# Layer-norm and post-norm ends: statistics per half tile, moments of both tiles ahead of the second normalisation

## The chip, the cores and the metric

One core of one Trainium2 chip. The metric is device microseconds of one execution of the whole program. The kernel before takes 2635.37 us (median of 3 runs, 2634.71 to 2635.55).

## The reference

The program computes two stacks of two layers on 256 tokens of width 1024 (the second stack also carries 256 context tokens), all in float32. The first stack has three layer norms in each layer:

```python
x = layer_norm(ALPHA * x + 0.5 * swiglu(x, gate1, up1, down1), ln1_g, ln1_b)
x = layer_norm(ALPHA * x + hybrid_mixer(x, ..., w_out), ln2_g, ln2_b)
x = layer_norm(ALPHA * x + 0.5 * swiglu(x, gate2, up2, down2), ln3_g, ln3_b)

def layer_norm(x, g, b):
    mu = mean(x); var = mean((x - mu) ** 2)
    return (x - mu) * rsqrt(var + 1e-5) * g + b
```

The second stack adds a branch scaled by a root mean square, after its mixer and after its FFN, for each stream of tokens:

```python
x = x + gate * rms_norm(y, weight)       # rms_norm(y) = y * rsqrt(mean(y * y) + 1e-6) * weight
```

## The kernel before

The program is a chain of phases. A phase gives each engine its own instruction list; the lists are tied by semaphores, and a barrier of all engines closes it (line 205), so that the next phase starts when the last engine is done. Weights and activations of the large products are split into a high and a low float32r part, and each product is made of three: high by high, high by low, low by high.

256 tokens are two tiles of 128 (`TT`). The down product of an FFN phase (`down`, line 544) and the output product of a mixer (`out_phase`, line 1019) collect a tile of 128 tokens by 1024 columns in two PSUM banks of 512 columns: tile 0 in banks 0 and 1, tile 1 in banks 2 and 3. The last step of either goes tile by tile and bank by bank, three products of 512 columns to a bank, 12 in all; after the sixth and the twelfth it raises `tile_done`. This is the start of what is called an end here.

A **layer-norm end** (`ln_vector`, line 315, and `ln_scalar`, line 334) takes one tile after the other. VectorE waits for `tile_done`, takes `bn_stats` of both banks (line 319) and `bn_aggr` (321); ScalarE takes the square root (337); VectorE the reciprocal (323) and the shift -mean/std (326); then VectorE normalises bank 0 of the tile (327) and ScalarE bank 1 (339), both into `z`. Only then does VectorE turn to the statistics of tile 1. TensorE turns `z` by transposes (`turn_tensor`, 350), eight to a tile: the first four wait for VectorE's half (`z0_ready`), the last four for ScalarE's (`z1_ready`). With both tiles turned, ScalarE (343) and VectorE (331) write four pieces each of `x_T`, with gain and bias, and the barrier follows.

There are six such ends: layer by layer an FFN phase, a mixer's output phase and an FFN phase.

A **post-norm end** (`post_scalar`, 378; `post_scale`, 392; `post_add`, 401) has ScalarE square both banks of a tile with a sum (384), take the root (387), and after VectorE's reciprocal (396) scale bank 1 (389) while VectorE scales bank 0 (398). ScalarE comes to tile 1 after that. After the transposes VectorE adds eight pieces to `x_T` (404).

There are six of these too: two in `out_both_phase` and two in `ffn_both_phase` (one for each stream; the first stream's lies under the products of the second, which run on TensorE until its transposes are placed at a fixed place, `BEHIND`), one in `out_phase` and one in the last `ffn_phase`.

SyncE loads the first weights of the next phase (`load_ahead`, 224) during the end, and waits for them before the barrier.

Of the kernel before, what the change touches and what calls it, by code (L numbers as in the profile page):

```python
# [36 lines left out]
ALU = mybir.AluOpType  # L37
ACT = mybir.ActivationFunctionType
# [4 lines left out]
D = 1024  # L43
# [3 lines left out]
TT = S // P  # L47
# [3 lines left out]
BANK = 512  # L51
# [261 lines left out]


def ln_vector(dve, k, s, t, par_g, par_b):
    for tt in range(TT):
        dve.wait_ge(s["tile_done"], tt + 1)
        for n in range(2):
            dve.bn_stats(t.stats[:, tt, n, :], k.ps[:, 2 * tt + n, :]).then_inc(s["ln_stats"], 1)
        dve.wait_ge(s["ln_stats"], 2 * tt + 2)  # L320
        dve.bn_aggr(t.mv[:, tt, :], t.stats[:, tt, :, :]).then_inc(s["ln_mv"], 1)
        dve.wait_ge(s["ln_std"], tt + 1)
        dve.reciprocal(t.rstd[:, tt:tt + 1], t.std[:, tt:tt + 1]).then_inc(s["ln_rstd"], 1)
        dve.wait_ge(s["ln_rstd"], tt + 1)

        dve.scalar_tensor_tensor(t.shift[:, tt:tt + 1], t.mv[:, tt, 0:1], -1.0, t.rstd[:, tt:tt + 1], ALU.mult, ALU.mult).then_inc(s["ln_shift"], 1)
        dve.tensor_scalar(t.z[:, tt, 0:BANK], k.ps[:, 2 * tt, :], t.mv[:, tt, 0:1], t.rstd[:, tt:tt + 1], ALU.subtract,
                          ALU.mult).then_inc(s["z0_ready"], 1)
    for f in (2, 3, 6, 7):
        dve.wait_ge(s["ln_turned"], f // 2 + 1)  # L330
        dve.tensor_scalar(k.x_T[:, f, 0:S], turned(k, f), par_g(f), par_b(f), ALU.mult, ALU.add)


def ln_scalar(act, k, s, t, par_g, par_b):
    for tt in range(TT):
        act.wait_ge(s["ln_mv"], tt + 1)
        act.activation(t.std[:, tt:tt + 1], t.mv[:, tt, 1:2], ACT.Sqrt, bias=k.eps[:, 0:1]).then_inc(s["ln_std"], 1)
        act.wait_ge(s["ln_shift"], tt + 1)
        act.activation(t.z[:, tt, BANK:D], k.ps[:, 2 * tt + 1, :], ACT.Identity, bias=t.shift[:, tt:tt + 1],
                       scale=t.rstd[:, tt:tt + 1]).then_inc(s["z1_ready"], 1)  # L340
    for f in (0, 1, 4, 5):
        act.wait_ge(s["ln_turned"], f // 2 + 1)
        act.activation(k.x_T[:, f, 0:S], turned(k, f), ACT.Identity, bias=par_b(f), scale=par_g(f))


def turned(k, f, bank=4):
    return k.ps[:, bank + f // 2, f % 2 * S:(f % 2 + 1) * S]
# [30 lines left out]
def post_scalar(act, k, s, t, st=0):  # L378
    if st == 0:
        act.activation(t.shift[:, 0:1], k.eps[:, 1:2], ACT.Sqrt)  # L380
    for tt in range(TT):
        made, at = st * TT + tt + 1, 4 * st + 2 * tt
        act.wait_ge(s["tile_done"], made)
        act.activation(t.z[:, tt, :], k.ps[:, at:at + 2, :].rearrange("p b n -> p (b n)"), ACT.Square,
                       accum_out=t.mv[:, tt, 0:1]).then_inc(s["po_sq"], 1)
        act.wait_ge(s["po_sq"], made)
        act.activation(t.std[:, tt:tt + 1], t.mv[:, tt, 0:1], ACT.Sqrt, bias=k.eps[:, 1:2], scale=1.0 / D).then_inc(s["po_std"], 1)
        act.wait_ge(s["po_r"], made)
        act.activation(t.z[:, tt, BANK:D], k.ps[:, at + 1, :], ACT.Copy, scale=t.rstd[:, tt:tt + 1]).then_inc(s["z1_ready"], 1)


def post_scale(dve, k, s, t, st=0):
    for tt in range(TT):
        made, at = st * TT + tt + 1, 4 * st + 2 * tt
        dve.wait_ge(s["po_std"], made)
        dve.reciprocal(t.rstd[:, tt:tt + 1], t.std[:, tt:tt + 1]).then_inc(s["po_r"], 1)
        dve.wait_ge(s["po_r"], made)
        dve.tensor_scalar(t.z[:, tt, 0:BANK], k.ps[:, at, :], t.rstd[:, tt:tt + 1], None, ALU.mult).then_inc(s["z0_ready"], 1)


def post_add(dve, k, s, gain, cols, st=0, bank=4):
# [27 lines left out]
def ffn_phase(nc, k, w_gate, w_up, w_down, src, ln=None, conv=None, post=None, mod=None, loaded=None, ahead=(), reloads=False):  # L429
# [17 lines left out]
    LAST = NF - 1  # L447
    PAIRS = (NF - 8) // 2
    with ExitStack() as ctx:
# [18 lines left out]
        with phase(nc, names) as (block, s):  # L468
# [49 lines left out]
            def _(pe):  # L518
# [25 lines left out]
                def down(t, n, first=False, end=False):  # L544
                    pe.wait_ge(s["dn_split"], t + 1)
                    pe.wait_ge(s["h_ready"], t + 1)
                    for tt in range(TT):
                        for c in range(2):
                            for p, (h, wt) in enumerate(((h_hi, dn_hi), (h_hi, dn_lo), (h_lo, dn_hi))):
                                last = pe.matmul(k.ps[:, 2 * tt + c, :], h[n][:, tt * P:(tt + 1) * P], wt[n][:, c * BANK:(c + 1) * BANK],  # L550
                                                 start=(first and p == 0), stop=(end and p == 2), skip_group_check=True)
                        if end:
                            last.then_inc(s["tile_done"], 1)
                    if not end:
                        last.then_inc(s["down_done"], 1)

# [462 lines left out]
def out_phase(nc, k, chunks, ln=None, post=None, ahead=(), stream=None, raw=None):  # L1019
# [5 lines left out]
    LAST = len(chunks) - 1  # L1025
    SLOTS = 3
    with ExitStack() as ctx:
# [4 lines left out]
        t = ln_buffers(nc, ctx)  # L1032
        if stream is not None:
            chunks = [(y, raw[:, n % SLOTS, :]) for n, y in enumerate(chunks)]
        with phase(nc, names) as (block, s):

            @block.sync
            def _(sp):
                if stream is not None:
                    for n in range(SLOTS):  # L1040
                        sp.sem_inc(s[f"w{n}_in"], 16)
                    for n in range(SLOTS, len(chunks)):
                        sp.wait_ge(s["lo_made"], n - SLOTS + 1)
                        sp.dma_start(raw[:, n % SLOTS, :], stream[n]).then_inc(s[f"w{n % SLOTS}_in"], 16)
                load_ahead(sp, s, ahead)

            @block.tensor
            def _(pe):
                if ln:
                    for tt in range(TT):  # L1050
                        for f in range(FT):
                            pe.matmul(k.ps[:, 2 * tt + f // 4, f % 4 * P:(f % 4 + 1) * P], k.x_T[:, f, tt * P:(tt + 1) * P],
                                      k.alpha[:, :], start=(f % 4 == 0), stop=False, skip_group_check=True)
                for n, (y, _) in enumerate(chunks):
                    rows, m = y.shape[0], n % SLOTS
                    pe.wait_ge(s["lo_made"], n + 1)
                    for tt in range(TT):
                        for c in range(2):
                            for p, (a, b) in enumerate(((y_hi, w_hi), (y_hi, w_lo), (y_lo, w_hi))):
                                last = pe.matmul(k.ps[:, 2 * tt + c, :], a[0:rows, m, tt * P:(tt + 1) * P], b[0:rows, m, c * BANK:(c + 1) * BANK],  # L1060
                                                 start=(n == 0 and p == 0 and not ln), stop=(n == LAST and p == 2), skip_group_check=True)
                        if n == LAST:
                            last.then_inc(s["tile_done"], 1)
                    if n < LAST:
                        last.then_inc(s["chunk_done"], 1)
                turn_tensor(pe, k, s, t.z, s["ln_turned"] if ln else s["po_turned"])

            @block.scalar
            def _(act):
                for n, (y, moving) in enumerate(chunks):  # L1070
                    rows, m = y.shape[0], n % SLOTS
                    if n >= SLOTS:
                        act.wait_ge(s["chunk_done"], n - SLOTS + 1)
                    act.activation(y_hi[0:rows, m, :], y, ACT.Copy)
                    if stream is not None:
                        act.wait_ge(s[f"w{m}_in"], n // SLOTS * 16 + 16)
                    act.activation(w_hi[0:rows, m, :], moving, ACT.Copy).then_inc(s["hi_made"], 1)
                if ln:
                    ln_scalar(act, k, s, t, *ln)
                else:  # L1080
                    post_scalar(act, k, s, t)

            @block.vector
            def _(dve):
                for n, (y, moving) in enumerate(chunks):
                    rows, m = y.shape[0], n % SLOTS
                    dve.wait_ge(s["hi_made"], n + 1)
                    dve.tensor_tensor(y_lo[0:rows, m, :], y, y_hi[0:rows, m, :].bitcast(F32), ALU.subtract)
                    dve.tensor_tensor(w_lo[0:rows, m, :], moving, w_hi[0:rows, m, :].bitcast(F32), ALU.subtract).then_inc(s["lo_made"], 1)
                if ln:  # L1090
                    ln_vector(dve, k, s, t, *ln)
                else:
                    post_vector(dve, k, s, t, *post)
# [1978 lines left out]
```

## Time and profile before

| | before |
|---|---|
| median of 3 runs | 2635.37 us |
| the profiled execution, its time | 2632.28 us |
| its span | 2630.5 us |
| mean granted clock of TensorE | 0.937 of full |
| TensorE busy | 2389.3 us (91%) |
| VectorE busy | 1317.9 us (50%) |
| ScalarE busy | 1135.1 us (43%) |
| GpSimd busy | 140.4 us (5%) |

The span is the profiled execution from its first to its last instruction; its own time has 1.8 us more around it. Busy times overlap. A granted clock of 1.00 is 2.4 GHz, one of 0.5 is 1.2 GHz, and a mean between them says how a stretch is shared between the two.

### The profile page before, as it was taken

How to read it: one execution, taken by the hardware profiler on the slowest of the kernel's cores; microseconds unless marked ns; L12 is line 12 of the kernel's file. 1: busy time of each engine (PE TensorE's matmuls, PEld its weight loads, DVE VectorE, ACT ScalarE, POOL GpSimd, SP SyncE). 2: the span in 40 equal slices, each digit the busy share in tenths (PEclk: the TensorE clock that was granted, in tenths of full speed). 3: DMA queues.
4: the chain of work that ended last, by engine and by line, in shares of the span. 5: the costliest groups of instructions: out<-in, count | busy, mean ns of one | idle time of the engine just before them, and what ended most of it. 6: DMA issues, size and time to landing. Idle time of an engine off the chain costs nothing. (4 is left out here: it accounts for less than half of the span.)

```text
span 2630.5 us, 42098 instructions
## 1 busy us (share of the span) xinstructions
PE 2389.3 (91%) x16488; PEld 2060.9 (78%) x16488; DVE 1317.9 (50%) x2144; ACT 1135.1 (43%) x1996; POOL 140.4 (5%) x177
## 2 busy tenths in 40 slices
PE   7998989998999899999688998769999988986998
PEld 6887978887989787888556887548888777865997
DVE  5443246444544315544444666555555554436665
ACT  3333244333433325443336576434334444434554
POOL 1000001000100000100000212110000000001000
PEclk9999889999999979999799999879999978997999
DMA  7876124885778421587311111124444252204663
GB/s 225 262 247 183 35 65 137 241 251 147 240 248 256 113 65 48 167 254 241 110 39 41 41 50 50 33 61 123 120 120 120 98 143 80 89 1 119 189 180 95
DMA packets 395292, 350.37 MB, mean 133 GB/s; under 512 B 25380, under 2 KB 358552, under 8 KB 394648
## 3 DMA queue, kind: packets, MB, share of 16 engines
q1 hardware_dynamic: 385076, 297.87, 39.4%
q10 hardware_dynamic: 10084, 50.66, 5.4%
q8 instruction: 93, 1.52, 0.2%
q14 instruction: 39, 0.32, 0.0%
HBM read 347.44 MB, written 1.05 MB: 132 GB/s over the span
## 5 line engine op out<-in xcount | busy, mean ns | idle before, releaser
L524 PE MATMUL ps<-x_hi,gu_hi 128*128 128x256 f32 x1680 | 478.9, 285 | 0.0
L524 PE MATMUL ps<-x_hi,gu_lo 128*128 128x256 f32 x1680 | 475.8, 283 | 0.0
L524 PE MATMUL ps<-x_lo,gu_hi 128*128 128x256 f32 x1680 | 475.8, 283 | 0.0
L524 PEld LDWEIGHTS ps<-x_hi,gu_hi 128*128 128x128 f32 x1680 | 322.2, 192 | 22.6 <-DVE gu_lo L669 17.5
L524 PEld LDWEIGHTS ps<-x_lo,gu_hi 128*128 128x128 f32 x1680 | 322.4, 192 | 2.6
L524 PEld LDWEIGHTS ps<-x_hi,gu_lo 128*128 128x128 f32 x1680 | 322.4, 192 | 0.0
L669 DVE TENSOR_TENSOR gu_lo<-w_gu,gu_hi 128x1024 fp32r<-128x1024 f32 x220 | 266.8, 1248 | 87.2 <-ACT gu_hi L600 87.2
L600 ACT ACTIVATE gu_hi<-w_gu 128x1024 fp32r<-128x1024 f32 x220 | 221.9, 1051 | 44.5 <-issue 30.1
L611 ACT ACTIVATE silu<-ps 128x256 f32<-128x256 f32 x88 | 33.7, 383 | 418.0 <-PE ps L524 405.0
L695 DVE SCALAR_TENSOR_TENSOR hid<-silu,ps 128x256 f32<-128x256 f32 x88 | 37.1, 421 | 316.0 <-ACT silu L611 315.8
L550 PE MATMUL ps<-dn_hi,h_hi 128*128 128x512 f32 x440 | 173.8, 395 | 5.9 <-DVE h_lo L704 5.8
L550 PE MATMUL ps<-dn_lo,h_hi 128*128 128x512 f32 x440 | 173.1, 394 | 0.0
L550 PE MATMUL ps<-dn_hi,h_lo 128*128 128x512 f32 x440 | 172.0, 391 | 0.0
L677 DVE TENSOR_TENSOR dn_lo<-w_dn,dn_hi 128x1024 fp32r<-128x1024 f32 x110 | 133.7, 1219 | 10.7 <-ACT dn_hi L604 10.7
L820 PE MATMUL ps<-both_x_lo,gu_hi 128*128 128x512 f32 x336 | 130.8, 389 | 0.0
L820 PE MATMUL ps<-both_x_hi,gu_lo 128*128 128x512 f32 x336 | 130.8, 389 | 0.0
L820 PE MATMUL ps<-both_x_hi,gu_hi 128*128 128x512 f32 x336 | 130.8, 389 | 0.0
L604 ACT ACTIVATE dn_hi<-w_dn 128x1024 fp32r<-128x1024 f32 x110 | 115.1, 1051 | 17.3 <-PE ps L550 17.3
L550 PEld LDWEIGHTS ps<-dn_hi,h_hi 128*128 128x128 f32 x440 | 83.3, 189 | 21.4 <-issue 7.0
L978 DVE SCALAR_TENSOR_TENSOR conv<-ps,par,conv 128x510 f32<-128x510 f32 x44 | 30.9, 745 | 134.4 <-ACT conv L915 134.4
L550 PEld LDWEIGHTS ps<-dn_hi,h_lo 128*128 128x128 f32 x440 | 83.1, 189 | 18.1
L550 PEld LDWEIGHTS ps<-dn_lo,h_hi 128*128 128x128 f32 x440 | 83.4, 189 | 13.4
(419 smaller groups left out, 5191.1 us busy)
## 6 DMA issues: line engine op xcount, KB each, us to landing
w_gu<-in_ffn_w_up SPq DMA_DIRECT2D x178, 512.0 KB, 6.2
w_dn<-in_ffn_w_down SPq DMA_DIRECT2D x134, 512.0 KB, 3.8
w_mod<-in_w_mod ACTq DMA_DIRECT2D x64, 768.0 KB, 6.1
w_gu<-in_ffn_w_gate SPq DMA_DIRECT2D x90, 512.0 KB, 5.1
odd_w<-in_odd_w_qkv SPq DMA_DIRECT2D x24, 512.0 KB, 5.2
w_gu<-in_ffn_w_down SPq DMA_DIRECT2D x11, 1024.0 KB, 5.0
hgrn_w<-in_even_w_in SPq DMA_DIRECT2D x20, 512.0 KB, 3.9
w_in_q<-in_w_in SPq DMA_DIRECT2D x2, 3072.0 KB, 11.2
```

The source lines that it names most:

```text
L524: last = pe.matmul(gu(n)[:, a, :], wt[n][:, a, f, :], x[:, f, :], start=(f == 0 and p == 0), stop=(f == FT - 1 and p == 2), skip_group_che ...
L550: last = pe.matmul(k.ps[:, 2 * tt + c, :], h[n][:, tt * P:(tt + 1) * P], wt[n][:, c * BANK:(c + 1) * BANK], start=(first and p == 0), stop ...
L600: act.activation(gu_hi[n][:, a, :, :], wgu[n][:, a, :, :], ACT.Copy).then_inc(s["w_hi"], 1)
L604: act.activation(dn_hi[n][:, :], wdn[n][:, :], ACT.Copy).then_inc(s["w_hi"], 1)
L611: act.activation(sil[n][:, :], gu(n)[:, 0, :], ACT.Silu).then_inc(s["act_done"], 1)
L669: last = dve.tensor_tensor(gu_lo[n][:, a, :, :], wgu[n][:, a, :, :], gu_hi[n][:, a, :, :].bitcast(F32), ALU.subtract)
L677: dve.tensor_tensor(dn_lo[n][:, :], wdn[n][:, :], dn_hi[n][:, :].bitcast(F32), ALU.subtract).then_inc(s["dn_split"], 1)
L695: dve.scalar_tensor_tensor(hid[n][:, :], sil[n][:, :], 0.5, gu(n)[:, 1, :], ALU.mult, ALU.mult).then_inc(s["h_full"], 1)
L820: last = pe.matmul(gu(n, a), wt[n][:, a, f, :], x[:, f, :], start=(f == 0 and p == 0), stop=(f == FT - 1 and p == 2))
L978: dve.scalar_tensor_tensor(cv[n][:, a, :, 1:S], streams(n, a)[:, :, 0:S - 1], conv.tap(0, t, a), cv[n][:, a, :, 1:S], ALU.mult, ALU.add).t ...
```

## The change

For a layer-norm end, `tile_done` is raised after each bank (four times) and VectorE's list gets another order: the statistics of both banks of tile 0 as they come, the moments of tile 0, the statistics of bank 0 of tile 1, reciprocal and shift of tile 0, statistics of bank 1 of tile 1, the moments of tile 1, and then the normalisation of tile 0, reciprocal and shift of tile 1, its normalisation. ScalarE's order stays as it was. For a post-norm end, `tile_done` stays as it was, and bank 1 of tile 0 is scaled by VectorE, behind bank 0, and not by ScalarE; tile 1 is as before. The post-norm functions serve all six ends.

```diff
 def ln_vector(dve, k, s, t, par_g, par_b):
-    for tt in range(TT):
-        dve.wait_ge(s["tile_done"], tt + 1)
-        for n in range(2):
-            dve.bn_stats(t.stats[:, tt, n, :], k.ps[:, 2 * tt + n, :]).then_inc(s["ln_stats"], 1)
+    def stats(tt, n):
+        dve.wait_ge(s["tile_done"], 2 * tt + n + 1)
+        dve.bn_stats(t.stats[:, tt, n, :], k.ps[:, 2 * tt + n, :]).then_inc(s["ln_stats"], 1)
+
+    def moments(tt):
         dve.wait_ge(s["ln_stats"], 2 * tt + 2)
         dve.bn_aggr(t.mv[:, tt, :], t.stats[:, tt, :, :]).then_inc(s["ln_mv"], 1)
+
+    def scales(tt):
         dve.wait_ge(s["ln_std"], tt + 1)
         dve.reciprocal(t.rstd[:, tt:tt + 1], t.std[:, tt:tt + 1]).then_inc(s["ln_rstd"], 1)
         dve.wait_ge(s["ln_rstd"], tt + 1)
 
         dve.scalar_tensor_tensor(t.shift[:, tt:tt + 1], t.mv[:, tt, 0:1], -1.0, t.rstd[:, tt:tt + 1], ALU.mult, ALU.mult).then_inc(s["ln_shift"], 1)
+
+    def first_half(tt):
         dve.tensor_scalar(t.z[:, tt, 0:BANK], k.ps[:, 2 * tt, :], t.mv[:, tt, 0:1], t.rstd[:, tt:tt + 1], ALU.subtract,
                           ALU.mult).then_inc(s["z0_ready"], 1)
+    for n in range(2):
+        stats(0, n)
+    moments(0)
+    stats(1, 0)
+    scales(0)
+    stats(1, 1)
+    moments(1)
+    first_half(0)
+    scales(1)
+    first_half(1)
...
@@ post_scalar
-        act.wait_ge(s["po_r"], made)
-        act.activation(t.z[:, tt, BANK:D], k.ps[:, at + 1, :], ACT.Copy, scale=t.rstd[:, tt:tt + 1]).then_inc(s["z1_ready"], 1)
+        if tt == TT - 1:
+            act.wait_ge(s["po_r"], made)
+            act.activation(t.z[:, tt, BANK:D], k.ps[:, at + 1, :], ACT.Copy, scale=t.rstd[:, tt:tt + 1]).then_inc(s["z1_ready"], 1)
...
@@ post_scale
         dve.tensor_scalar(t.z[:, tt, 0:BANK], k.ps[:, at, :], t.rstd[:, tt:tt + 1], None, ALU.mult).then_inc(s["z0_ready"], 1)
+        if tt < TT - 1:
+            dve.tensor_scalar(t.z[:, tt, BANK:D], k.ps[:, at + 1, :], t.rstd[:, tt:tt + 1], None, ALU.mult).then_inc(s["z1_ready"], 1)
...
@@ ffn_phase, down (out_phase alike, with n == LAST)
-                        if end:
-                            last.then_inc(s["tile_done"], 1)
+                            if end and (ln or c == 1):
+                                last.then_inc(s["tile_done"], 1)
```

## Rows read from the trace of the kernel before

**Rows 1.** What TensorE waited for before the transposes (line 356): us, times.

```profile
  DVE ln_z_b L327: 44.6, 24
  DVE ln_z_b L398: 18.1, 14
```

**Rows 2.** Timeline, first layer-norm end: start us, us, engine, line, operation [idle before].

```profile
229.37 0.39 PE L550 MATMUL ps<-dn_hi,h_lo 128*128 128x512 f32 x1
...
229.80 1.30 DVE L319 BATCH_NORM_STATS2 ln_stats_b<-ps 128x6 f32<-128x512 f32 x2 [2.36 <-PE ps L550]
...
230.73 0.39 PE L550 MATMUL ps<-dn_hi,h_lo 128*128 128x512 f32 x1
231.13 0.21 DVE L321 BATCH_NORM_AGGREGATE ln_mv_b<-ln_stats_b 128x2 f32<-128x12 f32 x1
231.37 0.29 ACT L337 ACTIVATE ln_std_b<-ln_mv_b,eps 128x1 f32<-128x1 f32 x1 [3.09 <-DVE ln_mv_b L321]
231.70 0.16 DVE L323 RECIPROCAL ln_rstd_b<-ln_std_b 128x1 f32<-128x1 f32 x1 [0.36 <-ACT ln_std_b L337]
231.90 0.16 DVE L326 SCALAR_TENSOR_TENSOR ln_shift_b<-ln_mv_b,ln_rstd_b 128x1 f32<-128x1 f32 x1
231.97 0.81 DVE L327 TENSOR_SCALAR ln_z_b<-ps,ln_mv_b,ln_rstd_b 128x512 f32<-128x512 f32 x1
...
232.70 1.28 DVE L319 BATCH_NORM_STATS2 ln_stats_b<-ps 128x6 f32<-128x512 f32 x2
...
232.83 1.09 PE L356 MATMUL ps<-ident,ln_z_b 128*128 128x128 f32 x8 [1.72 <-DVE ln_z_b L327]
...
234.86 0.81 DVE L327 TENSOR_SCALAR ln_z_b<-ps,ln_mv_b,ln_rstd_b 128x512 f32<-128x512 f32 x1
...
235.72 1.09 PE L356 MATMUL ps<-ident,ln_z_b 128*128 128x128 f32 x8 [1.79 <-DVE ln_z_b L327]
```

**Rows 3.** Timeline, fifth layer-norm end: its transposes, tile 0 and tile 1.

```profile
1062.68 1.91 PE L356 MATMUL ps<-ident,ln_z_b 128*128 128x128 f32 x8 [1.72 <-DVE ln_z_b L327]
...
1065.57 1.97 PE L356 MATMUL ps<-ident,ln_z_b 128*128 128x128 f32 x8 [0.98 <-DVE ln_z_b L327]
```

**Rows 4.** Stretches of four ends: from:to length, busy by engine, clock, DMA, GB/s.

```profile
229.76:238.55 8.79, 3.54 (x22) 2.49 (x21) 6.90 (x16) 4.08 (x8) 0.00 (x0) 1.00 0.01 2
425.91:435.19 9.28, 4.42 (x22) 3.20 (x21) 6.90 (x16) 4.07 (x8) 0.00 (x0) 0.79 0.00 0
...
861.04:869.83 8.79, 3.54 (x22) 2.49 (x21) 6.91 (x16) 4.07 (x8) 0.00 (x0) 0.91 0.00 0
1059.60:1068.89 9.29, 5.24 (x23) 3.86 (x21) 6.91 (x16) 4.07 (x8) 0.00 (x0) 0.67 0.00 0
```

**Rows 5.** The stretch right after the first end, same columns.

```profile
238.60:250.00 11.40, 9.01 (x18) 4.57 (x19) 6.33 (x11) 6.59 (x11) 0.00 (x0) 0.70 0.77 278
```

**Rows 6.** Timeline, post-norm end of `out_both_phase`, second stream.

```profile
1733.41 0.39 PE L2859 MATMUL ps<-both_w_hi,both_y_lo 128*128 128x512 f32 x1
...
1733.62 0.29 ACT L387 ACTIVATE ln_std_b<-ln_mv_b,eps 128x1 f32<-128x1 f32 x1
...
1734.15 0.69 ACT L389 ACTIVATE ln_z_b<-ps,ln_rstd_b 128x512 f32<-128x512 f32 x1 [0.23 <-DVE ln_rstd_b L396]
...
1734.73 1.02 ACT L384 ACTIVATE ln_z_b<-ps 128x1024 f32<-128x1024 f32 x1
...
1736.39 0.75 DVE L398 TENSOR_SCALAR ln_z_b<-ps,ln_rstd_b 128x512 f32<-128x512 f32 x1
```

**Rows 7.** Timeline, three other post-norm ends: a hidden turn, and the squares of tile 1.

```profile
1718.27 1.91 PE L356 MATMUL ps<-ident,ln_z_b 128*128 128x128 f32 x16
...
2136.59 1.02 ACT L384 ACTIVATE ln_z_b<-ps 128x1024 f32<-128x1024 f32 x1 [0.36 <-PE ps L870]
...
2615.95 1.02 ACT L384 ACTIVATE ln_z_b<-ps 128x1024 f32<-128x1024 f32 x1 [0.20 <-PE ps L550]
```

**Rows 8.** Waits of SyncE's queue, 636 to 656 us: total, times, longest.

```profile
SPq L205 <- PEq L205: 3.3, 1, 3.3
```

More of the change, by code:

```diff
@@ L334, in ln_scalar, with deviation, second_half @@
 def ln_scalar(act, k, s, t, par_g, par_b):
-    for tt in range(TT):
+    def deviation(tt):
         act.wait_ge(s["ln_mv"], tt + 1)
         act.activation(t.std[:, tt:tt + 1], t.mv[:, tt, 1:2], ACT.Sqrt, bias=k.eps[:, 0:1]).then_inc(s["ln_std"], 1)
+    def second_half(tt):
         act.wait_ge(s["ln_shift"], tt + 1)
@@ L340, in ln_scalar @@
                        scale=t.rstd[:, tt:tt + 1]).then_inc(s["z1_ready"], 1)
+    for tt in range(TT):
+        deviation(tt)
+        second_half(tt)
     for f in (0, 1, 4, 5):
@@ L1061, in _ @@
                                                  start=(n == 0 and p == 0 and not ln), stop=(n == LAST and p == 2), skip_group_check=True)
-                        if n == LAST:
-                            last.then_inc(s["tile_done"], 1)
+                            if n == LAST and (ln or c == 1):
+                                last.then_inc(s["tile_done"], 1)
                     if n < LAST:
```

## The prediction

> **What bounds the kernel now.** I read the page's busy times first: TensorE is busy 91% of the span, no other engine above 50%, so a stage counts where TensorE has nothing to do. The list of what TensorE waited for before its transposes gives the place: 44.6 us for VectorE's half in layer-norm ends and 18.1 us in post-norm ends [rows 1]. (It counts weight loads and matmuls separately, so about half of that is wall time.) Then the timeline of one end and the stretches of four of them. In the timeline the reader is to see one chain that passes from engine to engine with nothing beside it. From tile 0's last product at 229.76 (229.37 + 0.39) to the last product at 231.12, VectorE starts statistics only at 229.80, having sat idle 2.36 us, and takes them up for tile 1 at 232.70, although that tile has been finished since 231.12 [rows 2]. An end lasts 8.8 to 9.3 us from there to its last write, at 1.00 and 0.91 of the clock 8.79, at 0.79 and 0.67 some 9.28 [rows 4]. Nothing else of the program runs meanwhile, so what the chain loses there the program loses.
>
> **Layer-norm ends, step by step.** Call T the end of the last product, 231.12 here. One bank is three products, 0.68 us (12 of them take 2.72 us by the distance of 1.36 us between 229.37 and 230.73 for six). So the banks are done at T-2.04, T-1.36, T-0.68 and T. Durations from [rows 2]: statistics 0.68 each; two back to back take 1.30, so the second starts 0.62 after the first, 0.06 to 0.07 before that one ends; moments 0.21, root 0.29, reciprocal and shift 0.16, half normalisation 0.81, with VectorE's next instruction 0.73 after its start; a result passes on in 0.03 to 0.04. The new list, as times from T:
>
> - statistics of bank 0 at -2.01, of bank 1 at -1.32 (its bank lands at -1.36) to -0.64; moments -0.60 to -0.39; ScalarE's root -0.36 to -0.07.
> - statistics of bank 2 at -0.46 to 0.23; reciprocal 0.16, shift 0.36, statistics of bank 3 at 0.44 to 1.12.
> - moments of tile 1 at 1.15 to 1.36; ScalarE has normalised bank 1 from 0.55 to 1.33 and does the second root at 1.39 to 1.68.
> - VectorE normalises bank 0 at 1.29 to 2.10; reciprocal 2.02, shift 2.22, bank 2 at 2.30 to 3.11. ScalarE's bank 3 runs 2.42 to 3.20 and is wanted only by the fifth transpose.
>
> Before, the two halves of VectorE ended at T+1.66 and T+4.55, and tile 1's transposes began at 235.72, T+4.60 [rows 2]. After, tile 0's begin at T+2.15, 0.44 later than before, and eight of them take 0.94 us from first to ninth start (1.09 less 0.27 for the last one's own length, over seven, is 0.117 each); tile 1's begin at T+3.15. That is 1.45 us earlier. Everything behind (four pieces on each of ScalarE and VectorE, barrier) is the same, so an end gains 1.45 us at full clock. The two added waits on `tile_done` have nothing queued behind them that could run sooner: each bank's statistics are VectorE's next work. Two more semaphore increments on products cost nothing visible; the one after the sixth product leaves the stream's distance at 0.23 us as elsewhere. That VectorE's next free moment at T+2.02 is 0.3 us after the second root is the part not gained. Bounds for an end: if nothing overlaps on VectorE, 1.0 (below); at the other end, tile 0's turn as early as before (T+1.71) and tile 1's right behind it, at T+2.65, 1.95 earlier than before.
>
> Where the granted clock is low, transposes take 1.91 and 1.97 us for eight, 0.235 each [rows 3]. In the fifth end both tiles were slow: tile 0's eight would run from T+2.15 to T+4.03, and tile 1's start then and not at T+4.60, a gain of 0.57. In the second, third and sixth end only tile 1's were slow, and it costs such an end 0.49 us (9.28 against 8.79) [rows 4]; a turn that ends 1.45 us earlier escapes some of it, if the clock falls at the same moment. I take 0.25 for each of three, with ends 0 and 0.5. Sum: 5 x 1.45 + 0.57 + 0.75 = 8.6 us.
>
> **Post-norm ends.** ScalarE's second tile of squares starts at 1734.73, only because ScalarE first scaled bank 1 of tile 0; tile 1's last product ended at 1733.80 (1733.41 + 0.39) [rows 6]. Without that scaling the squares start at about 1733.84, and tile 1's root is ready at 1735.27 instead of 1736.16 (0.23 ahead of 1736.39, where tile 1's scaling starts). VectorE now scales both banks of tile 0: at 1734.15 and, with the same overlap of 0.07 as its normalisation, 1734.83, and is free at 1735.51. It reaches tile 1's reciprocal then, and its half at 1735.71 instead of 1736.39: 0.68 us gained, the other 0.2 eaten by the added instruction. Tile 0's fifth transpose waits until 1735.6 for the half that moved; with tile 1's at 1736.5 that is covered. The end of `out_phase` has the same times and gains 0.68 as well. The other four give nothing. In the second stream of `ffn_both_phase` and in the last FFN, ScalarE waited for TensorE before tile 1's squares, 0.36 and 0.20 us [rows 7]: it was free already. In the first streams of the two both-phases, the turn starts with no wait behind the other stream's products, all sixteen at once (1718.27 [rows 7]). Sum 1.4 us, ends 0 (if VectorE's second scaling delays as much as ScalarE's removal gains) and 1.8 (two times 0.89).
>
> **Is it passed on?** SyncE waits for the next phase's weights before the barrier; in the third end these had landed 3.3 us before the others came [rows 8], more than the 1.45 to 1.95 us that the others now come earlier; the sixth is alike, and the others had more by the same view. What the next phases issue goes from their start and moves with it.
>
> **The queue's overlap, against the Trainium skill.** The rows show the second statistics 0.62 us after the first, at a length of 0.68, and statistics 0.73 after a normalisation of 0.81 [rows 2]. The Trainium skill (VectorE: DVE Perf Modes, "The DRAIN you can't avoid") says that the next VectorE instruction does not start until the pipe is empty. With each instruction at full length, as by that rule, the list above is 0.46 us longer and an end gains 1.0, six ends 2.8 us less than forecast. I go by the rows; the rule is the first rival.
>
> **The clock.** The granted clock was 1.00 through the first end and 0.70 in the 11.4 us after it [rows 4, 5], and below 1.00 in the other three ends shown [rows 4]: it falls in or behind them. TensorE's idle stretch between last product and first transpose grows from 1.7 to 2.2 us, the one between the two turns nearly goes, and the whole end shrinks. I book nothing for either; the third and fourth rival hold the two sides.
>
> **The sum.** 8.6 + 1.4 = 10.0 us off the profiled execution's 2632.3. That execution lies 3.1 us below the median; the difference carries over, 2635.4 - 10.0 = 2625.4.
>
> **Rivals.**
> 1. No overlap on VectorE, the drain as stated: six ends lose 0.46, two lose 0.2, gain 6.8, 2628.6 us. Against it [rows 2] with two different pairs; for it, that reciprocal behind statistics is a pair that no row shows.
> 2. Half of it is hidden by something that doesn't move: weights that land late at a barrier, or the next phase's first work waiting on its own loads. Gain 4 to 5, 2631 us. For it: SyncE's margin in the third end is only 3.3 us. Against: it is a margin still.
> 3. Slower: the clock. TensorE idles 0.44 us longer before tile 0's transposes, the clock falls behind each of six ends one stretch more than it did, and the next phase's first products run at half speed. After the first end the low share is 0.30/0.5 of 11.4 us, 6.8 us, and half of that time is lost if TensorE is the bound: 3.4 us an end [rows 5], 20.5 in all, 2646 us. It is slower than before from a loss of 1.7 us an end (10.0 over six). Against: four of the six ends run partly at low clock anyway (0.79 and 0.67 in two of those shown), and their cost is already in the time; the three timed executions lie within 0.84 us.
> 4. The ends that ran at low clock come out at full clock once they are shorter: 0.5 us on four ends and 3.4 after one or two of them, 2619 us.
>
> **Numbers.** About 0.2% (5.3 us) is what a measurement tells from no change. Chances: forecast 0.66, no overlap 0.10, half hidden 0.12, clock worse 0.04, clock better 0.08. The forecast's bounds are 6 x 1.0 + 0 = 6 to 6 x 1.95 + 1.8 = 13.5 us, of which I hold 7 to 13 likely. The range 2620.5 to 2631.0 leaves out the clock rivals and half of the second. Faster than 2630.1: 0.85, within 0.2%: 0.11, slower than 2640.6: 0.04.
>
> **What would show it.** In the changed kernel's timeline of a layer-norm end: four statistics, the first about 0.68 us before tile 0's last product; VectorE's first half ending near T+2.1 and the second near T+3.1, TensorE's second turn at T+3.15; the stretch from tile 0's last product to the last write 7.3 us for 8.79. In `out_phase`'s post-norm end: squares of tile 1 right behind the first root, the second turn 0.68 us earlier. Wrong it would be if tile 1's turn waited for ScalarE's half or for tile 0's transposes, if SyncE came last at a barrier, or if the mean clock fell below 0.93.

## The result and the profile after

The changed kernel takes 2617.83 us (median of 6 runs, 2613.33 to 2621.0), beside 2634.16 for the kernel before (6 runs, 2629.96 to 2635.55): ratio 0.9945, 95% interval 0.9934 to 0.9956, or 14.5 us less. Forecast were 10.0 us less and a time of 2625.4 in a range of 2620.5 to 2631.0. The time lies below that range. Two later comparisons of the same two kernels gave 0.9959 and 0.9971. This section and the next say which part of the 14.5 us the change made.

| | before | after |
|---|---|---|
| profiled execution | 2632.28 us | 2618.02 us |
| its span | 2630.5 us | 2615.9 us |
| mean granted clock | 0.937 | 0.942 |
| TensorE busy | 2389.3 us | 2380.4 us |
| VectorE busy | 1317.9 us | 1320.2 us |
| ScalarE busy | 1135.1 us | 1131.4 us |

What TensorE waited for ahead of the transposes, in the kernel after, answers to [rows 1]: us, times.

```profile
  DVE ln_z_b L332: 26.8, 12
  DVE ln_z_b L419: 13.4, 14
  DVE ln_z_b L421: 0.7, 3
```

44.6 us became 26.8 (layer norm) and 18.1 became 14.1 (post norm; line 421 is VectorE's new scaling of tile 0's bank 1); matmuls and weight loads are both counted. The timeline of the sixth layer-norm end of the kernel after shows how; it answers to [rows 2], with T = 1270.57.

```profile
1268.57 1.38 DVE L318 BATCH_NORM_STATS2 ln_stats_b<-ps 128x6 f32<-128x512 f32 x2 [1.68 <-PE ps L573]
...
1269.98 0.21 DVE L322 BATCH_NORM_AGGREGATE ln_mv_b<-ln_stats_b 128x2 f32<-128x12 f32 x1
1270.11 0.65 DVE L318 BATCH_NORM_STATS2 ln_stats_b<-ps 128x6 f32<-128x512 f32 x1
1270.18 0.39 PE L573 MATMUL ps<-dn_hi,h_lo 128*128 128x512 f32 x1
...
1270.67 0.14 DVE L326 RECIPROCAL ln_rstd_b<-ln_std_b 128x1 f32<-128x1 f32 x1
...
1270.92 0.69 DVE L318 BATCH_NORM_STATS2 ln_stats_b<-ps 128x6 f32<-128x512 f32 x1
...
1271.65 0.21 DVE L322 BATCH_NORM_AGGREGATE ln_mv_b<-ln_stats_b 128x2 f32<-128x12 f32 x1
1271.78 0.76 DVE L332 TENSOR_SCALAR ln_z_b<-ps,ln_mv_b,ln_rstd_b 128x512 f32<-128x512 f32 x1
1271.89 0.29 ACT L352 ACTIVATE ln_std_b<-ln_mv_b,eps 128x1 f32<-128x1 f32 x1
1272.45 0.15 DVE L326 RECIPROCAL ln_rstd_b<-ln_std_b 128x1 f32<-128x1 f32 x1
1272.59 2.08 PE L376 MATMUL ps<-ident,ln_z_b 128*128 128x128 f32 x16 [2.02 <-DVE ln_z_b L332]
...
1272.71 0.81 DVE L332 TENSOR_SCALAR ln_z_b<-ps,ln_mv_b,ln_rstd_b 128x512 f32<-128x512 f32 x1
```

The reader is to see VectorE without a pause of more than 0.04 us from 1268.57 on, and sixteen transposes as one group: tile 1's follow tile 0's without a wait. Tile 0's turn starts at T+2.02 (forecast 2.15). The first transpose of tile 1 starts at T+3.01 (forecast 3.15). Not all ends ran like this. The stretches of the first and the sixth end of the kernel after, from tile 0's last product to the last write, answer to [rows 4].

```profile
229.41:237.45 8.04, 4.70 (x23) 3.72 (x21) 6.07 (x16) 4.08 (x8) 0.00 (x0) 0.79 0.00 0
1269.21:1276.42 7.21, 3.44 (x22) 2.49 (x21) 6.08 (x16) 4.08 (x8) 0.00 (x0) 1.00 0.62 174
```

At a granted clock of 1.00 the end takes 7.21 us for 8.79 [rows 4]; where the clock was at half in part of it, 8.04. From T to the last write, the six layer-norm ends took 7.43, 7.93, 7.90, 7.43, 7.92 and 7.91 us before, and 6.68, 6.91, 6.28, 6.20, 6.33 and 5.85 after: 0.75, 1.02, 1.62, 1.23, 1.59 and 2.06 less, 8.3 in all.

The post-norm end of `out_both_phase`, second stream, in the kernel after, answers to [rows 6].

```profile
1723.22 0.29 ACT L407 ACTIVATE ln_std_b<-ln_mv_b,eps 128x1 f32<-128x1 f32 x1
1723.43 1.02 ACT L404 ACTIVATE ln_z_b<-ps 128x1024 f32<-128x1024 f32 x1
...
1723.75 0.75 DVE L419 TENSOR_SCALAR ln_z_b<-ps,ln_rstd_b 128x512 f32<-128x512 f32 x1
...
1724.41 0.74 DVE L421 TENSOR_SCALAR ln_z_b<-ps,ln_rstd_b 128x512 f32<-128x512 f32 x1
...
1725.07 0.15 DVE L417 RECIPROCAL ln_rstd_b<-ln_std_b 128x1 f32<-128x1 f32 x1
...
1725.26 0.75 DVE L419 TENSOR_SCALAR ln_z_b<-ps,ln_rstd_b 128x512 f32<-128x512 f32 x1
1726.07 1.09 PE L376 MATMUL ps<-ident,ln_z_b 128*128 128x128 f32 x8 [0.20 <-DVE ln_z_b L419]
```

ScalarE squares tile 1 right after tile 0's root, and VectorE then is the one that is late. The last product ended at 1723.39, tile 1's turn starts 2.68 after it, 3.40 before: 0.73 us gained, in the end of `out_phase` as well, and nothing (0.01 at most) in the other four.

For the last FFN's end that "nothing" holds only for this pair of traces. In both, the products of tile 1 ran at half clock there, 0.43 us apart and not 0.23, so that ScalarE had time to spare; in the kernel before:

```profile
2614.86 0.63 PE L550 MATMUL ps<-dn_lo,h_hi 128*128 128x512 f32 x1
2615.29 0.63 PE L550 MATMUL ps<-dn_hi,h_lo 128*128 128x512 f32 x1
```

From the last product to the last write this end takes 6.22 us in both. In the traces below in which these products ran at full clock it takes 7.10 with the post-norm functions of before (one trace) and 6.35 to 6.37 with the changed ones (six traces): there it gains 0.7 as well.

SyncE's margin in the third end answers to [rows 8]:

```profile
SPq L205 <- PEq L205: 1.6, 1, 1.6
```

It fell from 3.3 to 1.6 us (from 3.5 to 1.6 in the sixth end, 9.8 or more in the others) and still hid the weights.

So the ends are 8.3 + 1.5 = 9.7 us shorter. The span is 14.6 us shorter. The other 4.9 us come from the stages between, whose code the change does not touch.

### The profile page after: what moved, and what is told of

The parts are those of the page before. It is cut to its first block and busy times, and to the rows that moved or that the text cites. A ratio compares the mean times of both kernels' runs of the same rounds, so it can differ in the third digit from the quotient of the medians.

```text
span 2615.9 us, 42098 instructions
## 1 busy us (share of the span) xinstructions
PE 2380.4 (91%) x16488; PEld 2055.1 (79%) x16488; DVE 1320.2 (50%) x2150; ACT 1131.4 (43%) x1990; POOL 140.7 (5%) x177
```

## The experiments

Each timing is a ratio to the kernel before, run on the same chip, with its 95% interval. "Ends" is the sum, over all twelve, of the time from the last product to the last write, read from that kernel's trace and compared with the trace before. Two theories were put against each other: **A**, that the change gains in the ends and again between them, by the granted clock; **B**, that it gains what the ends get shorter, and the rest is the spread between executions.

### One half of the change at a time

First run: `ln_vector` and `tile_done` as changed, the post-norm functions as before (the diff is against the changed kernel).

```diff
 def post_scalar ...
-        if tt == TT - 1:
-            act.wait_ge(s["po_r"], made)
+        act.wait_ge(s["po_r"], made)
...
```

> The layer-norm part of the change alone; the post-norm functions are those of before. Theory A (the change gains what the ends themselves get shorter, 9.7 us by the two traces, of which 8.3 in the six layer-norm ends and 1.5 in the post-norm ends; what the measured 14 to 16 us have beyond it is the clock's doing between the ends, and goes with the layer-norm ends): six layer-norm ends sum to 8 us less than before, the time is 12 to 14 us under the kernel before. Theory B (only the ends count, the rest of the measured difference is spread between executions): 7 to 9 us under the kernel before.

Measured: 2622.79 us, ratio 0.9966 (0.9954 to 0.9978), 8.9 us less; ends 9.0 us less. Theory B's number; A's lowest, 12, lies at the edge of the interval (5.8 to 12.1).

Second run: the reverse, the post-norm functions as changed and all else as before.

```diff
...
 def post_scale ...
+        if tt < TT - 1:
+            dve.tensor_scalar(t.z[:, tt, BANK:D], k.ps[:, at + 1, :], t.rstd[:, tt:tt + 1], None, ALU.mult).then_inc(s["z1_ready"], 1)
```

> The post-norm part alone; the layer-norm ends are those of before. Both theories: the ends of out_both_phase's second stream and of out_phase 0.73 us shorter each, the other four unchanged, 1.5 us in all. Theory A: the granted clock's mean stays at 0.937 or so, time 1 to 3 us under the kernel before. Theory B: 1.5 us, with a spread of 2.

Measured: 2631.58 us, ratio 1.0 (0.9989 to 1.0012); ends 1.6 us less, of which 0.73 in each of the two ends named. The trace shows the effect, the timing can't: it is smaller than the interval's 3 us to either side.

### The changed kernel again

No edit.

> The changed kernel once more. Theory A: 14 to 16 us under the kernel before again, mean granted clock 0.942 to 0.945, and the stages between the ends are several us shorter in sum than before. Theory B: 9 to 12 us, and the stages between the ends sum to what they were, give or take 4 us.

Measured: 2620.85 us, ratio 0.9959 (0.9946 to 0.9972), 10.8 us less. The profiled execution took 2626.66 us, 8.6 more than that of the first comparison, with the same instructions. Its ends are 8.9 us shorter than before's; all that lies between them sums to 3.2 us more than before's. Two stages of identical code show where the difference of the two executions lies. First those of the first comparison's profile (the second block's first mixer up to its output phase, and its neighbourhood attention):

```profile
1276.42:1708.03 431.61, 355.20 (x3558) 285.91 (x3559) 240.18 (x442) 232.32 (x462) 54.82 (x66) 0.92 0.15 47
2132.07:2383.08 251.01, 223.53 (x1457) 190.96 (x1457) 112.47 (x184) 111.63 (x248) 3.06 (x3) 0.89 0.24 68
```

and the same two in the execution of this run:

```profile
1276.36:1711.64 435.28, 359.45 (x3558) 289.36 (x3559) 240.58 (x442) 231.88 (x462) 55.61 (x66) 0.91 0.15 47
2136.13:2391.15 255.02, 228.00 (x1457) 194.02 (x1457) 112.47 (x184) 111.62 (x248) 3.06 (x3) 0.86 0.23 67
```

The columns are the stretch, its length, busy times by engine, granted clock, DMA share and GB/s. VectorE and ScalarE worked the same to 0.4 us; TensorE was granted 0.92 and 0.89 of its clock in one, 0.91 and 0.86 in the other, was busy 4.2 and 4.5 us longer and the stages took 3.7 and 4.0 us longer. In the kernel before they took 433.75 and 253.67 us at 0.91 and 0.87, in between:

```profile
1284.68:1718.43 433.75, 357.13 (x3558) 286.59 (x3559) 239.71 (x441) 232.91 (x463) 54.71 (x66) 0.91 0.15 47
2142.77:2396.44 253.67, 227.52 (x1457) 193.42 (x1457) 112.46 (x184) 111.61 (x248) 3.06 (x3) 0.87 0.24 67
```

Of the 4.9 us that the first profile had beyond its ends, 2.1 and 2.7 are these two stages (the two mixers of the first stack, 2.8 us longer and 2.6 shorter than before's, cancel). The second execution of the same kernel has these two stages 1.5 and 1.4 us longer than before's, so the gain of the first doesn't go with the change each time.

A third time, with the further kernel below beside it:

> The changed kernel a third time, to tell how much of the first result (0.9945, 14.5 us) was the spread between executions. If the difference is the ends alone (8.9 to 9.7 us by its traces): ratio 0.9960 to 0.9966. If 3 us or more come from elsewhere each time: 0.9945 to 0.9953.

Measured: 2623.93 us, ratio 0.9971 (0.9961 to 0.9982), 7.6 us less; ends 10.1 us less. The ratio lies beyond both forecasts, on the side of the smaller gain. The three comparisons together have 20 executions of the changed kernel, mean 2621.7 us, and the four of this study 67 of the kernel before, mean 2632.3: 10.6 us less, give or take 1.9 (1.96 standard errors from the spread of either, 3.9 and 2.8 us).

That 1.9 takes all executions as alike, and for the changed kernel they aren't: its means in the three comparisons are 2617.7, 2622.1 and 2624.2 us, and the first and the third differ by 6.5 (give or take 2.7). Those of the kernel before lie between 2632.0 and 2633.3 in all four. So a comparison can differ from the next by more than its interval says, and the uncertainty of the 10.6 is larger than 1.9. The second and the third ran on different chips; whether that matters, no run tells.

### Ends lengthened again

Two spare statistics on VectorE, behind the last write of a layer-norm end:

```diff
     for f in (2, 3, 6, 7):
         dve.wait_ge(s["ln_turned"], f // 2 + 1)
         dve.tensor_scalar(k.x_T[:, f, 0:S], turned(k, f), par_g(f), par_b(f), ALU.mult, ALU.add)
+    for n in range(2):
+        dve.bn_stats(t.pad[:, n, :], k.ps[:, 2 * n, :])
...
```

> The changed kernel with two more statistics instructions of VectorE (1.3 us, written to a spare place, nothing left out) behind the last write of each layer-norm end: the ends get their old length back, but TensorE's transposes stay early. Theory A, if what the clock gives depends on how long an end is from products to products: gain over before falls to 3 us (0.4 of an end plus 1.5 of the post-norm ends), clock back at 0.937. Theory A, if it depends on TensorE's idle stretches ahead of and between the transposes: the gain stays at 14.5 - 7.8 = 6.7 us. Theory B: 9.7 - 7.8 = 2 us.

Measured: 2627.55 us, ratio 0.9985 (0.9975 to 0.9995), 3.9 us less. The ends up to the last write of `x_T` were 11.1 us shorter than before, since the transposes ran at full clock in four of six, and the padding made the following stages some 1.1 us longer each (207.3 to 208.4 in the one that varies least), by that estimate 6.5 in six: 4.6 less in all. Ends and padding account for the time. The interval, 1.3 to 6.6 us less, holds both B's 2 and the 3 of A's first form; it leaves out only the 6.7 of A's second, and that barely.

The same padding ahead of the normalisation:

```diff
     moments(1)
+    for n in range(2):
+        dve.bn_stats(t.pad[:, n, :], k.ps[:, 2 * n, :])
     first_half(0)
...
```

> The changed kernel with the same two spare statistics instructions of VectorE as in the run padded behind, but ahead of tile 0's normalisation: TensorE idles 1.3 us longer after the last product, and each layer-norm end is 1.3 us longer. Theory B (only the ends' lengths count, what lies between varies by the clock at random): turns at T+3.3 and T+4.3, ends 1.3 us longer, the same time as with the padding behind, 3 to 5 us under the kernel before. Third rival of the prediction (the idle stretch ahead of the first transposes drops the clock): slower than with the padding behind by several us, mean granted clock 0.935 or less.

Measured: 2630.2 us, ratio 0.999 (0.998 to 0.9999), 2.6 us less, where B said 3 to 5; ends 2.0 us less. TensorE waited 3.22 us instead of 2.02 for its first transpose:

```profile
649.12 2.08 PE L378 MATMUL ps<-ident,ln_z_b 128*128 128x128 f32 x16 [3.22 <-DVE ln_z_b L332]
```

No price of the longer idle stretch shows beyond the ends' own length: the mean clock over all executions was 0.940, that of the padding behind, on another chip, 0.940. What differs between the two runs stands in the ends, 11.1 less 6.5 against 2.0: in two of these ends both turns ran at half clock.

The kernel before with five spare statistics behind each layer-norm end, the edit as above with `range(5)` and banks 0 and 2 in turn:

> The kernel before with five spare statistics instructions of VectorE (3.1 us) behind the last write of each layer-norm end. Theory B: six ends 3 us longer each, some 17 to 19 us slower, the stages between unchanged. Theory A (longer ends also cost clock between them, 28 us less of low clock went with 9.7 us of shorter ends): 22 to 28 us slower, mean granted clock 0.932 or less.

Measured: 2651.81 us, ratio 1.0076 (1.0063 to 1.009), 20.0 us more. The padding is one group of 3.08 us, and the stages after it are 3.2 us longer where little else varies, 19 us in six:

```profile
1297.49 3.08 DVE L333 BATCH_NORM_STATS2 ln_pad_b<-ps 128x6 f32<-128x512 f32 x5
```

The ends up to the last write are another 0.8 us longer in its trace, because the last FFN's end took 7.10 us and not 6.22. Theory A's number was 22 to 28, B's 17 to 19; the measured 20.0 (16.6 to 23.7) lies between, and padding and ends together, some 20, meet it.

### What the order adds

The changed kernel with VectorE's old order; `tile_done` still tells the banks apart.

```diff
-    for n in range(2):
-        stats(0, n)
-    moments(0)
-    stats(1, 0)
-    scales(0)
-    stats(1, 1)
-    moments(1)
-    first_half(0)
-    scales(1)
-    first_half(1)
+    for tt in range(TT):
+        for n in range(2):
+            stats(tt, n)
+        moments(tt)
+        scales(tt)
+        first_half(tt)
```

> The changed kernel with VectorE's old order in the layer-norm ends (all of tile 0, then all of tile 1); each bank's products are still told apart, so the statistics of tile 0 run under tile 1's products. It shows what the early statistics give alone and what the order adds. Worked out: statistics of tile 0 end at T-0.64, so its whole chain runs 0.6 us earlier; tile 0's turn at T+1.1, tile 1's at T+4.0, an end 0.6 us shorter than before, 3.6 us in six, plus 1.5 of the post-norm ends: 5 us under the kernel before.

Measured: 2626.72 us, ratio 0.9978 (0.9969 to 0.9987), 5.8 us less; ends 6.2 us less. Tile 0's turn starts at T+1.12, tile 1's at T+4.00 (1274.55 + 0.39 = 1274.94 is T):

```profile
1274.55 0.39 PE L569 MATMUL ps<-dn_hi,h_lo 128*128 128x512 f32 x1
...
1276.05 1.09 PE L372 MATMUL ps<-ident,ln_z_b 128*128 128x128 f32 x8 [1.12 <-DVE ln_z_b L332]
...
1278.94 1.09 PE L372 MATMUL ps<-ident,ln_z_b 128*128 128x128 f32 x8 [1.79 <-DVE ln_z_b L332]
```

The early statistics are 0.60 of the 1.59 us by which tile 1's turn moved, the order 0.99. (In six ends 0.60 is 3.6 us; the trace has 4.9, since tile 1's transposes were slow in two of the ends and not in four as before.)

### A further step

ScalarE normalises both banks of tile 0, with its second root between them, and VectorE does tile 1's half.

```diff
     moments(1)
-    first_half(0)
     scales(1)
     first_half(1)
...
-    for tt in range(TT):
-        deviation(tt)
-        second_half(tt)
+    deviation(0)
+    act.wait_ge(s["ln_shift"], 1)
+    act.activation(t.z[:, 0, 0:BANK], k.ps[:, 0, :], ACT.Identity, bias=t.shift[:, 0:1],
+                   scale=t.rstd[:, 0:1]).then_inc(s["z0_ready"], 1)
+    deviation(1)
+    second_half(0)
+    second_half(1)
```

> A further step: in the layer-norm ends ScalarE normalises both banks of tile 0, its second root standing between the two, and VectorE goes from the moments of tile 1 straight to its reciprocal, shift and half. From the rows of the changed kernel: tile 0's turn starts at T+1.3 for 2.0 and waits at its fifth transpose until T+2.3; tile 1's starts at T+2.8 for 3.0 at full clock, and at T+3.3 for 3.7 to 3.8 where the clock is low. 0.2 to 0.45 us an end, 1.2 to 2.7 us under the changed kernel, 11 to 13 us under the kernel before. If the granted clock depends on TensorE's idle stretch, more.

Measured: 2618.55 us, ratio 0.9951 (0.9936 to 0.9965), 12.9 us less; ends 14.0 us less. The timeline of its sixth end, T = 1267.01:

```profile
1268.31 0.65 PE L379 MATMUL ps<-ident,ln_z_b 128*128 128x128 f32 x4 [1.30 <-ACT ln_z_b L359]
1268.33 0.29 ACT L351 ACTIVATE ln_std_b<-ln_mv_b,eps 128x1 f32<-128x1 f32 x1
1268.54 1.43 ACT L355 ACTIVATE ln_z_b<-ps,ln_shift_b,ln_rstd_b 128x512 f32<-128x512 f32 x2
1268.66 0.16 DVE L326 RECIPROCAL ln_rstd_b<-ln_std_b 128x1 f32<-128x1 f32 x1 [0.36 <-ACT ln_std_b L351]
...
1268.93 0.81 DVE L332 TENSOR_SCALAR ln_z_b<-ps,ln_mv_b,ln_rstd_b 128x512 f32<-128x512 f32 x1
1269.35 1.54 PE L379 MATMUL ps<-ident,ln_z_b 128*128 128x128 f32 x12 [0.38 <-ACT ln_z_b L355]
```

Turns start at T+1.30 and T+2.83; TensorE waits a second time, 0.38 us, for ScalarE's second bank. Again, beside the changed kernel:

> The kernel whose ScalarE normalises all of tile 0, once more and beside the changed kernel on one chip. Its ends are 14.0 us shorter than before's and 4 to 5 us shorter than the changed kernel's in the traces (by order alone 0.2 each, the rest by transposes that ran at full clock). Ends alone: ratio to before 0.9947 to 0.9960, 1 to 4 us under the changed kernel. If its transposes' full clock was luck: 1.2 to 2 us under it.

Measured: 2615.65 us, ratio 0.9932 (0.9916 to 0.9947), 17.9 us less; ends 13.8 us less. This version beats both kernels: 12 executions with a mean of 2616.8 us are 4.9 us (give or take 2.6, by the same reckoning as above) under the 20 of the changed kernel. The order of work gives 0.2 an end of that. The rest of the 4 us that its ends are shorter is transposes at full clock: tile 1's eight took 1.1 us or less in 9 of its 12 layer-norm ends and in 5 of 18 of the changed kernel. (In the two variants that leave tile 0's and tile 1's turns where the changed kernel has them, the layer-norm half alone and the padding behind, it was 2 and 4 of 6.)

The forecast of the second run was missed, though: 1 to 4 us under the changed kernel beside it. The two means are 9.2 us apart (give or take 2.9), the ends of the two traces 3.7. The two traced executions are 3.2 us apart, as their ends have it; but that of the changed kernel was its fastest of nine, 5.0 us under their mean. Whether the 5.5 us that the means have beyond the ends lie in slower ends of the other executions or between the ends, no trace shows.

## Why the prediction was right in its mechanism and wrong in its time

- **The layer-norm ends.** Forecast 8.6 us in six, measured 8.3 (and 7.5 and 8.8 in the other two profiles). The list of start times held to 0.16 us, those behind T all early: the reciprocal behind statistics and the normalisation behind moments were each a little shorter (0.14 for 0.16, 0.76 for 0.81), and two instructions of VectorE overlap by 0.08 us, where the prediction read 0.06 to 0.07 off rounded rows. At full clock an end gains 1.58 us.
- **Their clock.** Booked were one end with tile 0's transposes slow and 0.25 us gained in three others. Measured, both turns ran slow, at least in part, in the first two ends (gains of 0.75 and 1.02 us) and only the sixth ran fast throughout (2.06 for an end that had been slow). The sum came out the same because the errors cancelled, which is luck.
- **The post-norm ends.** Forecast 1.4 us, 0.68 in each of two and nothing in four; measured 1.5, 0.73 in each of those two. That the last FFN's end gains nothing was read from a trace in which its products ran at half clock; it is no property of the code.
- **Passed on.** Held: margins shrank, nothing came late, and rival 2 (half of the gain hidden) fell with it.
- **Rival 1 (no overlap on VectorE).** Fell. In the profile after the reciprocal starts at 1270.67, 0.09 before the statistics ahead of it end. The Trainium skill (VectorE: DVE Perf Modes, "The DRAIN you can't avoid") has the next instruction wait for the pipe to empty, and adds in the same paragraph that "A next op that is not held starts earlier"; the prediction took up only the first half. This trace fits the second half: where an instruction waits for nothing of the one ahead, it starts 0.08 us before that one ends.
- **Rival 3 (the clock, slower).** Fell with the result, 14.5 us less and not 11 more, and again with the padding ahead, which lengthened the idle stretch to 3.22 us at the same mean clock. **Rival 4 (clock better)** forecast 2619 for the reason that ends come out at full clock; in the changed kernel they did in one of six, so the first time lay near it for another reason.
- **The step that failed** is the last one: "the difference carries over, 2635.4 - 10.0 = 2625.4", with the range under it. The difference was right: 10.6 us over all three comparisons, 9.7 by the ends. Its base and its spread were not. Three executions within 0.84 us were read as the spread of the kernel, although the profiled one stood beside them, 3.1 us below their median; 67 of them lie between 2626.5 and 2637.9, with a mean of 2632.3. The base was 3.1 us high. The changed kernel's first six had a mean of 2617.7, 4.0 under the mean of all twenty. The two together make up 7.1 of the 7.6 us between 2625.4 and 2617.83, and the clause "the three timed executions lie within 0.84 us", used against rival 3, carried no weight. What moved the time beyond the ends is a term that the prediction put at nothing ("I book nothing for either", of the clock): in the first trace the stretches between the ends were 4.9 us shorter. Below the range's low edge, 2620.5, lie 8 of the 20 executions of the changed kernel.
- **What goes with the spread of the executions** is the granted clock in the four stages of the mixers: the stage of 251.01 us at 0.89 took 255.02 at 0.86. Whole executions fit this: where the mean clock is 0.001 higher, the time is 1.2 us shorter over 61 executions of the kernel before (correlation -0.69) and 1.4 over the 20 of the changed kernel (-0.89). No run here set the clock, so that it moves the time is not shown by experiment. Why it falls in one execution and not in another, and why the changed kernel's mean clock was 0.943 in the first comparison and 0.940 and 0.939 in the others, is open.

That a few us between the ends also go with the change (theory A) is not needed: in eleven comparisons the total differs from what the ends (and paddings) give by 0.1 to 4.8 us, to either side, by 0.4 more in the mean. A share of some 2 us can't be excluded, and the further version beside the changed kernel, 9.2 us apart for 3.7 in the ends, is not explained by theory B.

## What to carry to other kernels

At the end of a stage, write out what each engine does from the last product on, and move everything that needs only part of the products under the rest; then let the second tile's dependent chain start before the first tile's bulk work, and let whichever engine is free do that bulk. A sum of such steps can be right to 0.3 us in 10 (here partly by luck) and still miss the measured time: take the spread from many executions and more than one comparison, not from three executions, and judge a change of some tenths of a percent by the stretches it touches, in two traces.

## What the hardware showed unasked

- Executions of one program with the same instructions differed by up to 11 us in 2632 (67 of the kernel before) and 14 in 2622 (20 of the changed one), about 0.5%; between traces of one kernel mostly in the mixers' stages, where TensorE is busy 82 to 95% and its granted clock came out at 0.86 to 0.92.
- Two padded kernels with the same work, 1.2 us later or earlier in the end, had the same mean clock of 0.940: TensorE's idle stretch of 2.02 or 3.22 us in an end did not show in it.
- Of the ends whose transposes start 1.3 us after the last product, tile 1's ran at full clock in 9 of 12; of those that start 2.0 after it, in 11 of 30. That the earlier start is the reason is not shown: with the old order (starts at 1.1 and 4.0 us, and a wait between) it was 4 of 6.
